# Last two expert blocks of the second layer: from scatters to 0/1 matrix products inside the last norm

## The reference

```
def run(args):
    xblk, e = args
    return (jax.nn.silu(xblk @ w_gate[e]) * (xblk @ w_up[e])) @ w_down[e]
...
y = jnp.einsum('nkd,nk->nd', y_pairs, gate.astype(y_pairs.dtype))
...
x <- LayerNorm(alpha * x + sublayer(x))
```

## Time and profile before

| | |
|---|---|
| median of three runs (range) | 2638.08 us (2635.35 to 2639.31) |
| the profiled execution's own time | 2637.37 us |
| its span | 2635.5 us |
| TensorE, VectorE, ScalarE, GpSimd busy | 92%, 77%, 64%, 25% |
| mean granted clock of TensorE | 0.961 |
| last stretch, 2590 us to the end | 45.5 us |

### The profile page before, as it was taken

How to read it: one execution, slowest core, us unless ns; L and a number is a source line. 1 busy time by engine, 2 the same in 40 slices (tenths; PEclk the granted TensorE clock), 3 DMA queues, 4 the chain that set the end, 5 groups by cost and what they waited for, 6 DMA issues and landing times. The chain is left out here.

```text
span 2635.5 us, 37642 instructions
## 1 busy us (share of the span) xinstructions
PE 2425.9 (92%) x12633; PEld 2075.8 (79%) x12633; DVE 2027.5 (77%) x2598; ACT 1695.5 (64%) x1798; POOL 657.2 (25%) x486
## 2 busy tenths in 40 slices
PE   8989989987979999999999599998979999999992
PEld 8969968874867888888888489987867888888882
DVE  4788876677888889889888544446788889889885
ACT  3369846666227777777777466663157777777773
POOL 0105727732012212121221412120003222122123
PEclk9999999997989999999999699998979999999996
DMA  5502344215339699988898411105259699999994
GB/s 172 136 18 79 81 107 123 78 34 157 106 136 384 215 347 366 358 324 317 308 371 287 172 57 41 41 9 172 102 196 372 228 345 368 362 373 365 367 353 151
DMA packets 115278, 565.24 MB, mean 214 GB/s; under 512 B 23520, under 2 KB 27872, under 8 KB 65904
## 3 DMA queue, kind: packets, MB, share of 16 engines
q1 hardware_dynamic: 89776, 512.19, 53.4%
q0 software_dynamic: 25408, 51.84, 7.3%
HBM read 574.25 MB, written 74.34 MB: 246 GB/s over the span
## 5 line engine op out<-in xcount | busy, mean ns | idle before, releaser
L2083 DVE TENSOR_TENSOR e0wlo<-e0raw,e0whi 128x2048 fp32r<-128x2048 f32 x214 | 486.6, 2289 | 68.7 <-ACT e0whi L1938 68.7
L2083 DVE TENSOR_TENSOR e1wlo<-e1raw,e1whi 128x2048 fp32r<-128x2048 f32 x208 | 472.9, 2289 | 66.6 <-ACT e1whi L1938 66.6
L1938 ACT ACTIVATE e0whi<-e0raw 128x2048 fp32r<-128x2048 f32 x214 | 409.7, 1914 | 98.4 <-PE e0u L93 42.2
L1938 ACT ACTIVATE e1whi<-e1raw 128x2048 fp32r<-128x2048 f32 x208 | 397.9, 1915 | 94.6 <-PE e1u L93 40.4
L91 PE MATMUL odd_banks<-h2T_hi,odd_w_hi 128*128 128x348 f32 x480 | 171.6, 357 | 1.8 <-PEq L123 1.3
L92 PE MATMUL odd_banks<-h2T_lo,odd_w_hi 128*128 128x348 f32 x480 | 155.2, 323 | 0.0
L93 PE MATMUL odd_banks<-h2T_hi,odd_w_lo 128*128 128x348 f32 x480 | 154.8, 323 | 0.0
L91 PE MATMUL m_y<-m_whi,m_xhi 128*128 128x512 f32 (+1 forms) x304 | 123.4, 406 | 23.2 <-DVE m_wlo L1645 22.7
L93 PE MATMUL m_y<-m_whi,m_xlo 128*128 128x512 f32 (+1 forms) x304 | 120.4, 396 | 0.0
L92 PE MATMUL m_y<-m_wlo,m_xhi 128*128 128x512 f32 (+1 forms) x304 | 120.2, 395 | 0.0
L91 PE MATMUL e0g<-e0whi,e0xh 128*128 128x512 f32 x284 | 116.1, 409 | 3.6 <-DVE e0xl L2088 3.6
(11 more groups left out here) (488 smaller groups left out, 7053.0 us busy)
## 6 DMA issues: line engine op xcount, KB each, us to landing
e0raw<-in_moe_w_gate SPq DMA_DIRECT2D x72, 1024.0 KB
e0raw<-in_moe_w_up SPq DMA_DIRECT2D x72, 1024.0 KB
e0raw<-in_moe_w_down SPq DMA_DIRECT2D x72, 1024.0 KB
e1raw<-in_moe_w_gate SPq DMA_DIRECT2D x70, 1024.0 KB
e1raw<-in_moe_w_up SPq DMA_DIRECT2D x70, 1024.0 KB
e1raw<-in_moe_w_down SPq DMA_DIRECT2D x70, 1024.0 KB
qki_w_raw<-in_w_even SPq DMA_DIRECT2D x22, 512.0 KB
odd_w_raw<-in_w_odd SPq DMA_DIRECT2D x20, 512.0 KB, 3.5
```

Of the source, the lines that this page charges most:

```text
L1938: act.activation(w_hi[:, i, :], raw[:, i, :], ACT.Copy).then_inc(hi_done[i], 1)
L2083: dve.tensor_tensor(w_lo[:, i, :], raw[:, i, :], w_hi[:, i, :].bitcast(F32), ALU.subtract).then_inc(lo_done[i], 1)
```

## The change

Only the second layer changes. The last two blocks' outputs are no longer scattered.

- `Rest` is a tensor of four weight chunks that outlives the expert stage. During the stage it is the place of the split up weights (chunks 2 and 3); the other four chunks keep a tensor of the stage.
- In `last_turn` ScalarE writes the outputs of blocks m and m + 1, scaled, as fp32r high halves into `Rest` (L2041), and VectorE the low halves (L2200). VectorE also builds, in `keep`, a 0/1 matrix for each of the two blocks, 128 slots by 1024 tokens: 1 where the slot's token is that token (L2193).
- SyncE waits only for scatter m - 1, and then issues all eight row loads and the two gain loads inside the expert stage.
- `last_norm` takes the place of `combine` for this layer. TensorE multiplies the 0/1 matrices with the kept outputs, eight matmuls for each block of 128 rows, into one of two pairs of PSUM banks; VectorE adds the loaded rows and takes the sum over the row in the same instruction (L2579). GpSimd divides it to the mean (L2629); ScalarE squares with an accumulated sum (L2605) and takes the root (L2607); VectorE subtracts the mean and multiplies with the gain (L2584), takes the reciprocal (L2586); ScalarE scales (L2612); GpSimd adds the bias (L2633), VectorE scales and adds it for the last block (L2599).
- `combine` loses its branches for the last layer; for the first nothing changes in it.

```diff
+class Rest:
+
+
+    def __init__(self, c, name):
+        self.up = c.sb(name + "_wu", [P, 4, EXPERT_CHUNK], F32R)
+
+    def w_hi(self, i):
+        return self.up[:, i - 2, :]
+
+    def w_lo(self, i):
+        return self.up[:, i, :]
+
+    def y_hi(self, e):
+        return self.up[:, 0, e * D:(e + 1) * D]
+
+    def y_lo(self, e):
+        return self.up[:, 2, e * D:(e + 1) * D]
+
+    def place(self, e):
+        return self.up[:, 1 + 2 * e, 0:T]
...
-def experts(nc, name, const, picks, h_d, sum_d, wg_d, wu_d, wd_d, first, raw, sums):
+def experts(nc, name, const, picks, h_d, sum_d, wg_d, wu_d, wd_d, first, raw, sums, rest=None):
...
-        w_hi, w_lo = c.sb(name + "whi", [P, NCH, CH], F32R), c.sb(name + "wlo", [P, NCH, CH], F32R)
+        n_own = NCH if rest is None else NCH - 2
+        own_hi, own_lo = c.sb(name + "whi", [P, n_own, CH], F32R), c.sb(name + "wlo", [P, n_own, CH], F32R)
+
+        def chunk(i, own, kept):
+            if rest is None:
+                return own[:, i, :]
+            return kept(i) if i in (2, 3) else own[:, i if i < 2 else i - 2, :]
+
+        w_hi = [chunk(i, own_hi, rest and rest.w_hi) for i in range(NCH)]
+        w_lo = [chunk(i, own_lo, rest and rest.w_lo) for i in range(NCH)]
+        tok_f, tok_n, gate2 = c.sb(name + "_tf", [P, 2]), c.sb(name + "_tn", [P, 2, NB - 1]), c.sb(name + "_g2", [P, 2])
...
+        def last_y(e, j):
+            return y_ps[:, j, :] if e == 0 else (g_ps, u_ps)[j][:]
...
-            sp.wait_ge(lo_done[1], m + 3)
-            sums.load_gains(sp)
-            sp.wait_ge(y_stored, m * 16 + 32)
-            sums.load_rows(sp, BEFORE_CHANGE)
+            if rest is None:
+                sp.wait_ge(lo_done[1], m + 3)
+                sums.load_gains(sp)
+                sp.wait_ge(y_stored, m * 16 + 32)
+                sums.load_rows(sp, BEFORE_CHANGE)
+            else:
+                sp.wait_ge(y_stored, m * 16)
+                for i in WU:
+                    sp.wait_ge(lo_done[i], m + 2)
+                sums.load_rows(sp, slice(0, 4))
+                sp.wait_ge(lo_done[1], m + 3)
+                sums.load_gains(sp)
+                sums.load_rows(sp, slice(4, 8))
...
-            last = pool.snap(m + 1)
-            pool.wait_ge(x_tr, m + 2)
-            pool.tensor_copy(ix[:], tok_i[:, bass.ds(last, 1)]).then_inc(ix_done, 1)
-            scatter(m)
...
+            if rest is None:
...
+            else:
+                pool.drain()
...
-                take_y(m)
-                act.wait_ge(y_mm, m + 2)
-                for j, ps in enumerate((g_ps, u_ps)):
-                    ins = act.activation(x[:, 512 * j:512 * j + 512], ps[:], ACT.Copy, scale=by_slot[:, bass.ds(m + 1, 1)])
-                ins.then_inc(y_taken, 1)
+                if rest is None:
...
+                else:
+                    act.wait_ge(kept, 1)
+                    for e in range(2):
+                        act.wait_ge(y_mm, m + 1 + e)
+                        for j in range(2):
+                            act.activation(rest.y_hi(e)[:, HALVES[j]], last_y(e, j), ACT.Copy, scale=gate2[:, e:e + 1]).then_inc(kept_hi, 1)
...
+                if rest is not None:
+                    keep(m)
+
+            def keep(m):
+                at = Chain(dve, at_chain)
+                dve.tensor_copy(gate2[:], by_slot[:, bass.ds(m, 2)]).then_inc(kept, 1)
+                at.link(dve.tensor_copy(tok_f[:], tok_i[:, bass.ds(m, 2)]))
+                for e in range(2):
+                    at.link(dve.tensor_scalar(tok_n[:, e, :], const[:, C_IB:C_IB + NB - 1], -1.0, tok_f[:, e:e + 1], ALU.mult, ALU.add))
+                    dve.tensor_tensor(rest.place(e)[:, 0:SEQ].rearrange("p (n j) -> p n j", j=P),
+                                      const[:, C_I128:C_I128 + P].rearrange("p (n j) -> p n j", n=1).broadcast_to([P, NB - 1, P]),
+                                      tok_n[:, e, :].rearrange("p (n j) -> p n j", j=1).broadcast_to([P, NB - 1, P]), ALU.is_equal
+                                      ).then_inc(kept, 1)
+                for e in range(2):
+                    for j in range(2):
+                        dve.wait_ge(kept_hi, 2 * e + j + 1)
+                        dve.scalar_tensor_tensor(rest.y_lo(e)[:, HALVES[j]], last_y(e, j), gate2[:, e:e + 1],
+                                                 rest.y_hi(e)[:, HALVES[j]].bitcast(F32), ALU.mult, ALU.subtract).then_inc(kept, 1)
+                dve.wait_ge(kept, 7)
...
-def combine(nc, name, const, sums, out_d, hT_hi, hT_lo, beside=None, odd=None):
+def combine(nc, name, const, sums, out_d, hT_hi, hT_lo, beside, odd):
...
+def last_norm(nc, name, const, sums, rest, out_d):
+
+
+    blocks, x = sums.blocks, sums.rows
+    N = len(blocks)
+    with Ctx(nc) as c:
+        stat, junk, eps = c.sb(name + "st", [P, N, 5]), c.sb(name + "junk", [P, D]), c.sb(name + "eps", [P, 1])
+        TOTAL, MEAN, VAR, STD, RSTD = range(5)
+        g_ps, b_ps = c.ps(name + "g", [P, 2, 512]), c.ps(name + "b", [P, 2, 512])
+        acc = [c.ps(name + f"a{s}", [P, 2, 512]) for s in range(2)]
+        stored, bias_in, gain_in, eps_in, acc_mm, added, mean_done, square_done, root_done, scales, gained, scaled, normed, last_normed = (
+            c.sem(name + n) for n in ("so", "bin", "gin", "epi", "amm", "add", "mnd", "sqd", "rtd", "scl", "gnd", "scd", "nd", "lnd"))
+        block = c.block()
+
+        def col(n, a):
+            return stat[:, n, a:a + 1]
+
+        def flat(ps):
+            return ps[:].rearrange("p a n -> p (a n)")
+
+        @block.sync
+        def _(sp):
+            for n in range(N):
+                if n < N - 1:
+                    sp.wait_ge(normed, n + 1)
+                else:
+                    sp.wait_ge(last_normed, 1)
+                sp.dma_start(out_d[P * n:P * n + P, :], x(n)).then_inc(stored, 16)
+            sp.wait_ge(stored, 16 * N)
+
+        @block.tensor
+        def _(pe):
+            for n in range(N):
+                if n >= 2:
+                    pe.wait_ge(added, n - 1)
+                for j in range(2):
+                    for e in range(2):
+                        at = rest.place(e)[:, P * n:P * n + P]
+                        pe.matmul(acc[n % 2][:, j, :], at, rest.y_hi(e)[:, HALVES[j]], start=e == 0, stop=False)
+                        last = pe.matmul(acc[n % 2][:, j, :], at, rest.y_lo(e)[:, HALVES[j]], start=False, stop=e == 1)
+                last.then_inc(acc_mm, 1)
+
+        @block.vector
+        def _(dve):
+            def add(n):
+                dve.wait_ge(acc_mm, n + 1)
+                dve.wait_ge(sums.loaded[n], 16)
+                dve.tensor_tensor_reduce(x(n), flat(acc[n % 2]), x(n), 1.0, 0.0, ALU.add, ALU.add, col(n, TOTAL)).then_inc(added, 1)
+
+            def gain(n):
+                dve.wait_ge(mean_done, n + 1)
+                dve.wait_ge(square_done, n + 1)
+                dve.scalar_tensor_tensor(x(n), x(n), col(n, MEAN), flat(g_ps), ALU.subtract, ALU.mult).then_inc(gained, 1)
+                dve.wait_ge(root_done, n + 1)
+                dve.reciprocal(col(n, RSTD), col(n, STD)).then_inc(scales, 1)
+
+            dve.memset(eps[:], EPS / ALPHA ** 2).then_inc(eps_in, 1)
+            for n in range(N + 2):
+                if n < N:
+                    add(n)
+                if n == 2:
+                    dve.wait_ge(gain_in, 1)
+                if n >= 2:
+                    gain(n - 2)
+            dve.wait_ge(gained, N)
+            dve.wait_ge(scales, N)
+            dve.wait_ge(bias_in, 1)
+            dve.scalar_tensor_tensor(x(N - 1), x(N - 1), col(N - 1, RSTD), flat(b_ps), ALU.mult, ALU.add).then_inc(last_normed, 1)
+
+        @block.scalar
+        def _(act):
+            def square(n):
+                act.wait_ge(added, n + 1)
+                act.activation(junk[:], x(n), ACT.Square, scale=-float(D), bias=col(n, TOTAL), accum_out=col(n, VAR)).then_inc(square_done, 1)
+                act.wait_ge(square_done, n + 1)
+                act.activation(col(n, STD), col(n, VAR), ACT.Sqrt, scale=float(D) ** -3, bias=eps[:]).then_inc(root_done, 1)
+
+            def rescale(n):
+                act.wait_ge(gained, n + 1)
+                act.wait_ge(scales, n + 1)
+                act.activation(x(n), x(n), ACT.Copy, scale=col(n, RSTD)).then_inc(scaled, 1)
+
+            act.wait_ge(sums.gains_loaded, 32)
+            act.activation(flat(g_ps), sums.gain(0), ACT.Copy).then_inc(gain_in, 1)
+            act.wait_ge(eps_in, 1)
+            for n in range(N + 1):
+                if n < N:
+                    square(n)
+                if n == 0:
+                    act.activation(flat(b_ps), sums.gain(1), ACT.Copy).then_inc(bias_in, 1)
+                if n >= 2:
+                    rescale(n - 2)
+
+        @block.gpsimd
+        def _(pool):
+            def mean(n):
+                pool.wait_ge(added, n + 1)
+                pool.tensor_scalar(col(n, MEAN), col(n, TOTAL), 1.0 / D, None, ALU.mult).then_inc(mean_done, 1)
+
```

(45 more changed lines are left out.)

112 lines of the change are left out of this document (45 added, 67 removed).

## The result

| | before | after |
|---|---|---|
| median of the runs beside each other | 2636.72 us (2634.48 to 2639.31, 4 runs) | 2618.99 us (2618.04 to 2622.25, 4 runs) |
| ratio (95% interval) | | 0.9929 (0.9917 to 0.9941) |
| profiled execution, own time; span | 2637.37; 2635.5 us | 2618.86; 2617.1 us |

The account below looks back on a forecast made before the run. Bound: when GpSimd ends its last bias addition. Norm starts 10.0 us earlier, 6.0 goes back before the first bias addition, five shorter steps give 2.5: 6.5 less than 2637.37, so 2630.9 us, range 2628.0 to 2636.0.

Parts of the forecast that it names:

- Sum: GpSimd's last bias addition ends at 2623.0 against 2629.49 us, 6.5 us less.
- VectorE's last split ends: VectorE splits the last half of y after ScalarE's copy: 2590.34 + 0.69 + 0.1 = 2591.1 us.
- norm starts: Stage exit of 1.3 us after the last split: norm at 2592.4 against 2602.36, 10.0 us earlier.
- first addition ends: VectorE adds the first block's rows after waiting for TensorE's product at clock 0.50; done at 2597.6 us.
- first rescale ends, first bias addition starts: ScalarE's first rescale, after squares, table load, roots and bias copy, ends at 2605.4; GpSimd's first bias addition starts at 2605.55.
- steady block: Each norm block takes 2.55 us, with ScalarE, VectorE and GpSimd level; upper bound 3.0.
- last bias addition ends: GpSimd's bias addition of the seventh block, the point the sum goes to, ends at 2623.0 us.
- the drain: About 1.38 us beside ScalarE's 1.28 us table load by the skill; not added, it would make the result 2632.3.
- dear start: Fused add-and-reduce pays its first-use cost again, or exit stays 4.4: first addition 3.1 us later, 2634.0 us; chance 0.15.
- the row loads: Eight row loads and two gain loads, 5 MB, issued from about 2573 us, end before 2592 and cost nothing.
- The clock rival: TensorE's clock stays at 0.50 in the norm, 3.43 us per block's product: 2637.7 us, slower by 0.3; chance 0.08.
- the change only touches the last 50 us: Premise that only the kernel's end changes, so TensorE's 92% average busy time says nothing about the change.

Follow-up runs that it names:

- the run without the shift: Changed kernel with its three small tiles (tok_f, tok_n, gate2) allocated behind all others, so the token operands lie where they lay before: 2630.78 us, ratio 0.9972.
- the execution at half pace above: Changed kernel with the Sqrt table load and bias copy ahead of ScalarE's first square, one execution: 5261.86 us, TensorE at about half its pace throughout.
- the padding runs: Kernel before with unused SBUF tiles that move operands; in front of e0ix and e1ix, 64, 128 and 192 bytes gave 2634.31, 2626.93 and 2623.0 us.

## Why the prediction was wrong, and where it was right

**Right: the tail, almost to the digit.** Sum predicted 6.5 us; measured 6.6 from the closing copy on, in the changed kernel and in the run without the shift. That the latter's median is 2630.78 us against a forecast of 2630.9 is luck in the last digits: beside it the kernel before took 2638.55, not the 2637.37 from which the forecast subtracts, and the ratio's interval allows a gain of 5 to 10 us. By its steps, as distances from the closing copy:

| step | predicted | measured |
|---|---|---|
| VectorE's last split ends | 2.0 | 2.1 |
| norm starts | 3.3 | 3.6 (exit 1.5 instead of 1.3) |
| first addition ends | 8.5 | 8.7 |
| first rescale ends, first bias addition starts | 16.3, 16.5 | 16.5, 16.6 |
| steady block (rescale to rescale) | 2.55 | 2.50 |
| last bias addition ends | 33.9 | 33.75 |

The table load took 1.28 us and the root started 0.01 behind it, so the drain that the Trainium skill adds ("ScalarE: Activation LUTs", What ACT_TABLE_LOAD costs) again doesn't show. The fused operation took 1.23 us at its first use after a long pause: no dear start. The clock was 0.50 for the first block's product and half of the second's, 1.00 from there to the last; the row loads (5 MB) were hidden, although they took 9.3 us to land instead of 7.

**The clock rival** did not come. Its price, 0.3 us slower than before, is neither confirmed nor refuted: in the execution at half pace above a block took 3.75 us on average where the rival has 3.43, and its tail was 2.1 us longer than before's. With eight blocks shorter by 0.32 us that tail would be about 46 us, an estimate from these rows, level with the 46.4 of before. The rule of the Trainium skill ("TensorE: Matmul & The Clock Gate", HAM oscillation) held for the first burst alone. The bursts behind it hardly had waits between them: TensorE was busy 12.79 of the 13.50 us from 2586.3 to its last product, at a clock of 1.00.

**Wrong: a step that isn't in the sum.** The step that failed stands in the prediction's first paragraph: "the change only touches the last 50 us". With it failed the use of the profiled execution's time for all that lies before. "Only the second layer changes", in the section on the change, is wrong in the same way: the line of the diff that allocates `tok_f`, `tok_n` and `gate2` stands outside every `if`, so the first layer gets these tiles too. The change allocates 128 bytes in both layers' expert stages, and thereby moved the stationary operands of some 5,100 products from a bad distance (64) to a better one (192). That is worth 11.8 us by medians (2630.78 without the shift, 2618.99 with it), nearly twice the tail. The prediction had looked at added instructions, waits and DMAs, and took an allocation as free. No rival named it, so the range (2628.0 to 2636.0) did not reach 2618.99.

## What to carry to other kernels

The start-to-start time of a 128x512 fp32r product with its own weight load depends on where the stationary operand lies against the moving one modulo 256 bytes: 0.227 us at distance 0 for up and down products, 0.230 on average at 192, 0.232 at 128, 0.233 at 64, at a granted clock of 1.00 each time. Moving both by 128 bytes changes nothing; it is the only common shift that was tried. A list of durations shows it only as a median of 388 or 394 ns, which at first sight is noise. By the Trainium skill ("TensorE: Matmul & The Clock Gate", Step-by-step: what each phase is for) the two operands have read ports of their own, and loading the next weights takes nothing from the running product. By that rule the distance would make no difference; the padding runs disagree, by up to 6 ns in 233. What causes it stays open, and so does why gate products with the high weight half keep 0.230 to 0.231 at distance 0.

Where the clock falls after a pause is not told by the pause's length. After 3.7 us it was 1.00 at the restart and stayed there in one kernel, was 0.50 in another that was alike from the last expert product on, and fell 0.3 us behind the restart in a third (the seventh block's bias on VectorE). After 1.9 us it stayed at 1.00 once and fell 1.1 us behind the restart once. It is worth 1.7 us of the tail. And one execution in this study ran wholly at half TensorE's pace, while its granted clock reads 1.00.
